# Two mixers of a streaming encoder: three projection blocks between scores and transposes, the product with v one pair later

## The chip, the cores and the metric

The kernel runs on one core of a Trainium2 chip. The metric is the device time of one launch in microseconds, the median of three runs.

## The reference, cut to what matters

The input x is 256 rows of 1024 float32 values. Two layers follow each other; each is FFN, mixer, FFN, with a residual and a layer norm behind each of the three. Every norm needs the whole row, so nothing of the next stage can begin on a row before its norm is done.

```python
x = layer_norm(ALPHA * x + 0.5 * swiglu(x, ...))      # 1024 -> 2816 -> 1024
q, k, v = (x @ w_qkv) cut into 16 heads of 64
# layer 0: softmax(q k^T * scale + bias by clipped distance), band of 64-row chunks
# layer 1: a = sigmoid(z) * product of sigmoid(-z) over later keys, strictly causal
x = layer_norm(ALPHA * x + (a @ v) @ w_o)
x = layer_norm(ALPHA * x + 0.5 * swiglu(x, ...))
```

## The kernel before

Every large product is made in three matmuls for accuracy. A weight is read by DMA into one of four raw slots (L280, L310), ScalarE copies it to a rounded high part (`hi_part`, L605), VectorE subtracts to get the low part (`lo_part`, L773), and TensorE issues high by high, high by low and low by high (`three`, L354). A *unit* is 128x2048 weights; `unit_ready(n)` makes TensorE wait until the low part of unit n is there. Five slots hold the split weights, and a slot is written again once the unit before it in the same slot has been used (`unit_used`). x itself is turned by TensorE (`transpose_x`, L344) and split in the same way (`xT_hi_part` L640, `xT_lo_part` L803), in three pieces for each half of the rows.

In a mixer TensorE works through 24 projection blocks (`proj_block`: 24 matmuls of 128x128 by 256 columns each), 8 pairs of heads, and 16 half blocks of the output product (`out_half`: 6 matmuls of 512 columns). A v block covers 128 rows and all four heads of its group; a q or k block covers one pair of heads and all 256 rows. A block's result goes to one of two PSUM banks and ScalarE copies it out (`copy_proj`, L675); block i waits for the copy of block i - 2. All engines have one fixed order of work, written by hand; semaphores carry the rest.

For a pair of heads the steps are: `scores` (TensorE, L516, banks 0 and 1); then the weights: in mixer 0 VectorE adds the bias and takes the extremes (`soften`, L889), ScalarE takes the exponentials (L685), VectorE divides by the sums (`normalise`, L896 and L901); in mixer 1 ScalarE makes two sigmoids (L693, L696), GpSimd masks both (L1026), VectorE scans (L909) and multiplies (`break_sticks`, L916). Then `turn_probs` transposes the weights into the same two banks (TensorE, L526), ScalarE copies them out (`probsT_copy`, L702), `head_out` multiplies with v (TensorE, L537 and L538), and ScalarE and VectorE split the result (L706, L921).

The order on TensorE before: the blocks v00, v10, v01, v11, q00, k00, q01 (unit, then half), the first pair's scores, and for each pair

```python
scores(m, pp)
todo, turn = fillers(pp)
for j, block in enumerate(todo):
    if j == turn:
        turn_probs(m, pp)
    ...                      # proj_block or out_half
head_out(m, pp)
```

So two blocks lie between the scores and the transposes (three half blocks in the last two pairs), one behind them, and then the product with v of the same pair. Pair 5 has two projection blocks and one half block. VectorE begins a mixer with the norm and split of the second half of the rows (`norm(t - 1, 1, split_too=True)`, L816 to L839 and L803) and only then makes the low parts of the mixer's units 2, 3 and 4, in this order. Units 0 to 3 are v0, v1, q0 and k0; units 0 and 1 were split in the FFN before. When the output product is done, `finish` turns the first half of the new x.

Of the kernel before, what the change touches and what calls it, by code (L numbers as in the profile page):

```python
# [26 lines left out]
P = 128  # L27
SEQ, D, FF, HEADS, HD = 256, 1024, 2816, 16, 64
DEPTH = 2
ROWS = SEQ // P  # L30
# [38 lines left out]

FFN_SLOTS = [j % 4 for j in range(24)] + [4, 0, 1, 2, 3, 0, 4, 2, 3]  # L70
MIX_SLOTS = [0, 1, 4, 2, 3] + [4, 0, 1, 2, 3] * 2 + [4]
SLOT = (FFN_SLOTS + MIX_SLOTS + FFN_SLOTS) * DEPTH
assert len(SLOT) == UNITS and len(FFN_SLOTS) == UNITS_FFN and len(MIX_SLOTS) == UNITS_MIX


def former(n):
# [4 lines left out]

MIX_ORDER = ([("v", 0), ("v", 1), ("q", 0), ("k", 0), ("q", 1), ("k", 1)]
             + [(what, g) for g in range(2, GROUPS) for what in "vqk"] + [("o", g) for g in range(GROUPS)])

BLOCKS = [("v", 0, 0), ("v", 1, 0), ("v", 0, 1), ("v", 1, 1)]
for group in range(GROUPS):
    if group >= 2:
        BLOCKS += [("v", group, 0), ("v", group, 1)]
    BLOCKS += [(what, group, pair) for pair in range(2) for what in "qk"]
FIRST_BLOCKS = 7  # L90

AHEAD = [(6, 7), (8, 9), (10, 11), (12, 13), (14, None), (15, 16), (None, 17), (None, None)]
# [6 lines left out]
def build(nc, x_in, w_qkv, w_o, rel_bias, w_gate, w_up, w_down, ln_g, ln_b, table, out):  # L101
    with ExitStack() as ctx:
# [58 lines left out]
        Y = [[psum[:, 5, :], psum[:, 6, :]], [psum[:, 7, :], psum[:, 3, :]]]  # L161

# [5 lines left out]
        SCORES = psum[:, 0:2, 0:KEYS]  # L168
# [56 lines left out]
        def wait_block(eng, m, i):  # L225

            what, g, b = BLOCKS[i]
            if b == 0:
                eng.wait_ge(proj_done, m * 3 * GROUPS + sum(x[2] == 0 for x in BLOCKS[:i + 1]))
            else:  # L230
                eng.wait_ge(unit_used, MIX_UNIT[m] + MIX_ORDER.index((what, g)) + 1)

        def fillers(pp):


            o = [("o", g, r, half) for g in range(GROUPS) for r in range(ROWS) for half in range(2)]
            if pp < PAIRS - 2:
                at = FIRST_BLOCKS + 3 * pp
                return (BLOCKS[at:at + 3] + o)[:3], 2
            at = 4 * (pp - (PAIRS - 2)) + 1  # L240
            return o[at:at + 4], 3
# [85 lines left out]
        def _(pe):  # L327
# [77 lines left out]
            def half_block(r, half, d, n, count, ready=None):  # L405
# [3 lines left out]
                for kk in range(2):  # L409
# [3 lines left out]
                    last = three(Y[r][half], (hT_hi[:, k, rows], hT_lo[:, k, rows]),  # L413
# [51 lines left out]
            def proj_block(m, i, t=None, between=()):  # L465
# [10 lines left out]
                for k in range(KD):  # L476
# [3 lines left out]
                    if t is not None:  # L480
                        xT_ready(t, b, k)
# [8 lines left out]
            def out_half(m, g, r, half):  # L490

                n = MIX_UNIT[m] + 3 * GROUPS + g
                if half == 0:
                    unit_ready(n)
                if (g, r, half) == (0, 1, 1):

                    pe.wait_ge(proj_copied, (m + 1) * len(BLOCKS))

                last = half_block(r, half, g, n, GROUPS,
                                  lambda kk: pe.wait_ge(headout_lo, m * PAIRS + 2 * g + kk + 1))  # L500
# [5 lines left out]
            def scores(m, pp):  # L506
# [3 lines left out]
                if m * PAIRS + pp > 0:  # L510
                    pe.wait_ge(probsT_done, m * PAIRS + pp)
                q, k = qT[g % 2], kT[g % 2]
                for r, (a, b) in enumerate(SPANS):
                    for h in range(2):
                        part = slice(h * HD, (h + 1) * HD)
                        last = pe.matmul(SCORES[:, h, a:b], q[part, p, r * P:(r + 1) * P], k[part, p, 0:b - a],  # L516
                                         start=True, stop=True)
                last.then_inc(scores_done, 1)

            def turn_probs(m, pp):  # L520
                pe.wait_ge(probs_ready, m * PAIRS + pp + 1)
                pr = probs[pp % 2]
                for h in range(2):

                    for to, at in ((0, 2 * P), (P, 0), (2 * P, P)):
                        last = pe.transpose(SCORES[:, h, to:to + P], pr[:, h, at:at + P], ident[:])  # L526
# [15 lines left out]
            def mixer_matmul(m, t, finish):  # L542
# [4 lines left out]
                for i in range(3, FIRST_BLOCKS):  # L547
                    proj_block(m, i)
                for pp in range(PAIRS):
                    scores(m, pp)  # L550
                    todo, turn = fillers(pp)
                    for j, block in enumerate(todo):
                        if j == turn:
                            turn_probs(m, pp)
                        if block[0] == "o":
                            out_half(m, *block[1:])
                        else:
                            proj_block(m, BLOCKS.index(block))
                    head_out(m, pp)
                last_g = GROUPS - 1  # L560
                out_half(m, last_g - 1, 0, 1)
                for half in range(2):
                    out_half(m, last_g, 0, half)
                for half in range(2):
                    out_half(m, last_g - 1, 1, half)
                out_half(m, last_g, 1, 0)
                finish((0, 1))
                out_half(m, last_g, 1, 1)
# [26 lines left out]
        def _(act):  # L595
# [4 lines left out]
            def hi_part(n, raw_slot, count, slot, before):  # L600

                act.wait_ge(raw_loaded[raw_slot], count * 32)
                if before is not None:
                    act.wait_ge(unit_used, before + 1)
                act.activation(w_hi[slot][:], raw[raw_slot][:], ACT.Copy).then_inc(hi_done, 1)  # L605

            def hi_unit(n):
                if n < UNITS:
                    hi_part(n, n % RAW, n // RAW + 1, SLOT[n], former(n))
# [33 lines left out]
            def ffn_scalar(f, t):  # L643
# [8 lines left out]
                with act.Fori(0, CHUNKS // 2) as i:  # L652
                    for cc in (1, 2):
                        c = i * 2 + cc
                        silu(f, c - 1, 1, (cc - 1) % 2)
                        for kh in range(2):
                            j = 2 * cc + 2 + kh
                            n = n0 + j
                            hi_part(i * 4 + n, n % RAW, i + (n // RAW + 1), j % 4, i * 4 + (n - 4))
# [9 lines left out]
            def copy_proj(m, i):  # L669
                what, g, b = BLOCKS[i]  # L670
                wait_block(act, m, i)
                if g >= 2:
                    act.wait_ge(headout_done, m * PAIRS + 2 * (g - 1))
                dst = {"v": v, "q": qT, "k": kT}[what][g % 2]
# [14 lines left out]
            def sigmoids(m, pp):  # L689
# [3 lines left out]
                act.activation(stick[:], SCORES, ACT.Sigmoid, scale=-1.0).then_inc(sigmoid_done, 1)  # L693
                if pp >= 2:
                    act.wait_ge(probsT_psum, m * PAIRS + pp - 1)
                act.activation(probs[pp % 2][:], SCORES, ACT.Sigmoid).then_inc(sigmoid_done, 1)  # L696

            def probsT_copy(m, pp):
# [3 lines left out]
                act.activation(probsT[:], SCORES, ACT.Copy).then_inc(probsT_done, 1)  # L702
# [342 lines left out]
```

## Time and profile before

| | |
|---|---|
| median of the three runs | 1000.98 us (1000.14, 1000.98, 1001.07) |
| span of the profiled execution | 998.0 us |
| outside the span, against the median | 3.0 us |
| TensorE matmuls | 983.0 us busy, 98% of the span |
| VectorE | 571.9 us, 57% |
| ScalarE | 444.5 us, 45% |
| mixer 0 | from about 196.6 to 309 us |
| mixer 1 | from about 684.5 to 801 us |

For the profiled execution the page has the span from its first to its last instruction and no whole time of its own; the runs' times include what lies before and behind the span, 3.0 us by the median. Matmuls are pipelined and their ends are modelled, so this document compares the starts of matmuls: in a running block of 256-column matmuls they are 0.12 us apart, in a half block of 512 columns 0.23 us.

### The profile page before, as it was taken

The numbers are of one execution on the slowest core, as the hardware profiler recorded it, in microseconds if no ns is written. First come the engines' busy times: TensorE is split into PE (matmuls) and PEld (weight loads), VectorE is DVE, ScalarE is ACT, GpSimd is POOL, SyncE is SP. The second block draws the span as 40 slices with busy tenths as digits, with TensorE's granted clock in tenths as the row PEclk, the third lists the DMA queues.
The fourth block names the chain that finished last, engine by engine and source line by source line (L and its number), as shares of the span: only waits on it lengthen the run. The fifth ranks groups of instructions, "written<-read, shape, count | busy, mean of one in ns | idle before, by whom it ended". The sixth has DMA issues, their size and how long they took to land.

```text
span 998.0 us, 13263 instructions
## 1 busy us (share of the span) xinstructions
PE 983.0 (98%) x5158; PEld 826.3 (83%) x5158; DVE 571.9 (57%) x624; ACT 444.5 (45%) x507; POOL 44.7 (4%) x72
## 2 busy tenths in 40 slices
PE   9999999999999999999999999999999999999996
PEld 7888888899987888888888888889888678888885
DVE  5555463766557555554665554547576585445634
ACT  5443452357653444352254434534565443344430
POOL 1100000000001000000000000001121110000000
PEclk9999999999999999999999999999999999999999
DMA  9956546456633756546565565654554436564521
GB/s 319 290 185 194 199 174 220 166 182 225 211 114 90 247 169 196 188 172 243 169 211 168 180 198 197 225 174 154 180 196 142 127 124 210 181 201 168 210 85 43
DMA packets 136951, 182.80 MB, mean 183 GB/s; under 512 B 5936, under 2 KB 120784, under 8 KB 136912
## 3 DMA queue, kind: packets, MB, share of 16 engines
q1 hardware_dynamic: 134032, 173.56, 52.6%
q0 software_dynamic: 2592, 8.17, 2.6%
q8 instruction: 28, 0.46, 0.2%
q10 hardware_dynamic: 288, 0.52, 0.2%
q14 instruction: 11, 0.09, 0.0%
HBM read 181.16 MB, written 1.07 MB: 183 GB/s over the span
## 4 chain that ended last, share of the span: by engine, by line
PE 91%; DVE 5%; POOL 1%; issue 1%; ACT 1%; DMA 0%; POOLq 0%; SPq 0%; DVEq 0%
PE psum L356 28%; PE psum L358 28%; PE psum L357 28%; PE psum L393 2%; DVE stick L909 2%; PE psum L516 1%; PE psum L526 1%; POOL stick L1026 1%; PE psum L537 1%; PE psum L344 1%; DVE probs L916 1%; DVE stats L819 1%; DVE x L839 1%; DVE x L816 1%; ACT stick L693 1%
## 5 line engine op out<-in xcount | busy, mean ns | idle before, releaser
L773 DVE TENSOR_TENSOR w_lo<-raw,w_hi 128x2048 fp32r<-128x2048 f32 x162 | 368.8, 2287 | 158.0 <-ACT w_hi L605 157.5
L605 ACT ACTIVATE w_hi<-raw 128x2048 fp32r<-128x2048 f32 x162 | 303.0, 1907 | 89.5 <-PE psum L358 87.8
L356 PE MATMUL psum<-w_hi,xT_hi 128*128 128x512 f32 (+1 forms) x832 | 317.2, 381 | 0.7 <-DVE w_lo L782 0.7
L358 PE MATMUL psum<-w_hi,xT_lo 128*128 128x512 f32 (+1 forms) x832 | 310.9, 374 | 0.0
L357 PE MATMUL psum<-w_lo,xT_hi 128*128 128x512 f32 (+1 forms) x832 | 310.4, 373 | 0.0
L356 PEld LDWEIGHTS psum<-w_hi,xT_hi 128*128 128x128 f32 x832 | 156.7, 188 | 29.8 <-DVE w_lo L782 1.8
L358 PEld LDWEIGHTS psum<-w_hi,xT_lo 128*128 128x128 f32 x832 | 156.5, 188 | 28.3
L357 PEld LDWEIGHTS psum<-w_lo,xT_hi 128*128 128x128 f32 x832 | 156.9, 189 | 25.9
L356 PE MATMUL psum<-w_hi,hT_hi 128*128 128x512 f32 x416 | 164.3, 395 | 0.0
L358 PE MATMUL psum<-w_hi,hT_lo 128*128 128x512 f32 x416 | 162.1, 390 | 0.0
L357 PE MATMUL psum<-w_lo,hT_hi 128*128 128x512 f32 x416 | 162.0, 390 | 0.0
L629 ACT ACTIVATE gate_act<-psum 128x256 f32<-128x256 f32 x88 | 33.8, 384 | 255.8 <-PE psum L358 255.8
L790 DVE TENSOR_TENSOR hidden<-psum,gate_act 128x256 f32<-128x256 f32 x88 | 37.3, 424 | 161.6 <-ACT gate_act L629 161.6
L356 PEld LDWEIGHTS psum<-w_hi,hT_hi 128*128 128x128 f32 x416 | 78.1, 188 | 17.2 <-issue 1.7
L358 PEld LDWEIGHTS psum<-w_hi,hT_lo 128*128 128x128 f32 x416 | 78.1, 188 | 16.6
L357 PEld LDWEIGHTS psum<-w_lo,hT_hi 128*128 128x128 f32 x416 | 78.2, 188 | 15.5
L356 PE MATMUL psum<-xT_hi,w_hi 128*128 128x256 f32 x256 | 73.7, 288 | 0.0
L357 PE MATMUL psum<-xT_lo,w_hi 128*128 128x256 f32 x256 | 72.4, 283 | 0.0
L358 PE MATMUL psum<-xT_hi,w_lo 128*128 128x256 f32 x256 | 72.3, 283 | 0.0
L356 PEld LDWEIGHTS psum<-xT_hi,w_hi 128*128 128x128 f32 x256 | 49.0, 191 | 2.7 <-issue 2.0
L357 PEld LDWEIGHTS psum<-xT_lo,w_hi 128*128 128x128 f32 x256 | 49.1, 192 | 0.0
L358 PEld LDWEIGHTS psum<-xT_hi,w_lo 128*128 128x128 f32 x256 | 49.0, 192 | 0.0
(71 smaller groups left out, 512.2 us busy)
## 6 DMA issues: line engine op xcount, KB each, us to landing
raw<-in_ffn_w_down SPq DMA_DIRECT2D x88, 512.0 KB, 4.1
raw<-in_ffn_w_gate SPq DMA_DIRECT2D x86, 512.0 KB, 4.0
raw<-in_ffn_w_up SPq DMA_DIRECT2D x86, 512.0 KB, 5.0
raw<-in_w_qkv_a SPq DMA_DIRECT2D x24, 512.0 KB, 4.7
raw<-in_w_qkv_b SPq DMA_DIRECT2D x24, 512.0 KB, 4.5
raw<-in_w_o_a SPq DMA_DIRECT2D x8, 512.0 KB, 4.1
raw<-in_w_o_b SPq DMA_DIRECT2D x8, 512.0 KB, 3.7
gain<-in_ln_g POOLq DMA_DIRECT2D x6, 512.0 KB, 3.9
```

The lines of the kernel that those rows point to most:

```text
L344: last = pe.transpose(XT(piece)[:, (k - a) * P:(k - a + 1) * P], x[:, r, k * P:(k + 1) * P], ident[:])
L356: pe.matmul(acc, st[0], mv[0], start=first, stop=False)
L357: pe.matmul(acc, st[0], mv[1], start=False, stop=False)
L358: return pe.matmul(acc, st[1], mv[0], start=False, stop=last)
L393: last = pe.transpose(TURN[:, (2 * j + r) * P:(2 * j + r + 1) * P], hidden[:, r, j * P:(j + 1) * P], ident[:])
L516: last = pe.matmul(SCORES[:, h, a:b], q[part, p, r * P:(r + 1) * P], k[part, p, 0:b - a], start=True, stop=True)
L526: last = pe.transpose(SCORES[:, h, to:to + P], pr[:, h, at:at + P], ident[:])
L605: act.activation(w_hi[slot][:], raw[raw_slot][:], ACT.Copy).then_inc(hi_done, 1)
L629: act.activation(gate_act[:, r, :], GU[par][r][:, 0:CHUNK_F], ACT.Silu).then_inc(silu_done, 1)
L773: dve.tensor_tensor(w_lo[slot][:], raw[raw_slot][:], w_hi[slot][:], ALU.subtract).then_inc(lo_done, 1)
L790: dve.tensor_tensor(hidden[:, r, :], GU[par][r][:, CHUNK_F:], gate_act[:, r, :], ALU.mult).then_inc(hidden_done, 1)
L909: dve.tensor_tensor_scan(stick[:, h, ::-1], stick[:, h, ::-1], restart[:, ::-1], 1.0, ALU.mult, ALU.max).then_inc(stick_done, 1)
```

## The change

The order of blocks and pairs is now a table. Three blocks (or two blocks and two half blocks, or six half blocks) lie between a pair's scores and its transposes; behind the transposes come the product with v of the pair before, and the scores of the next pair. Scores alternate between banks 0, 1 and banks 5, 6, and the mixer's output accumulates in banks 7, 2, 3 and 1. Only four blocks stand ahead of the first scores: v00, v10, q00, k00. The units' order of arrival is unchanged up to index 5; later v of a group comes behind its q and k. Weight splits, copies and waits on ScalarE and VectorE are put in the new order.

```diff
+FIRST_BLOCKS = [("v", 0, 0), ("v", 1, 0), ("q", 0, 0), ("k", 0, 0)]
+DURING = [[("v", 0, 1), ("q", 0, 1), ("k", 0, 1)],
+          [("v", 1, 1), ("q", 1, 0), ("k", 1, 0)],
+          [("q", 1, 1), ("k", 1, 1), ("q", 2, 0)],
+          [("k", 2, 0), ("q", 2, 1), ("v", 2, 0)],
+          [("k", 2, 1), ("v", 2, 1), ("q", 3, 0)],
+          [("k", 3, 0), ("q", 3, 1), ("v", 3, 0)],
+          [("k", 3, 1), ("v", 3, 1), ("o", 0, 0, 0), ("o", 1, 0, 0)],
+          [("o", 0, 0, 1), ("o", 0, 1, 0), ("o", 0, 1, 1), ("o", 1, 0, 1), ("o", 1, 1, 0), ("o", 1, 1, 1)]]
+LAST_TURNED = [("o", 2, 0, 0)]
+LAST_OUT = [("o", 2, 0, 1), ("o", 3, 0, 0), ("o", 3, 0, 1), ("o", 2, 1, 0), ("o", 2, 1, 1), ("o", 3, 1, 0)]
...
-AHEAD = [(6, 7), (8, 9), (10, 11), (12, 13), (14, None), (15, 16), (None, 17), (None, None)]
+AHEAD = [(None, 5), (6, 7), (8, 9), (10, 11), (12, None), (13, 14), (15, 16), (17, None)]
...
+        Y_MIX = [[psum[:, 7, :], psum[:, 2, :]], [psum[:, 3, :], psum[:, 1, :]]]
...
-        SCORES = psum[:, 0:2, 0:KEYS]
+        SCORES = [psum[:, 0:2, 0:KEYS], psum[:, 5:7, 0:KEYS]]
...
                     if t is not None:
-                        xT_ready(t, b, k)
+                        xT_ready(t, b if what == "v" else 1, k)
...
-                if m * PAIRS + pp > 0:
-                    pe.wait_ge(probsT_done, m * PAIRS + pp)
+                if pp >= 2:
+                    pe.wait_ge(probsT_done, m * PAIRS + pp - 1)
...
                 proj_block(m, 2, t)
-                for i in range(3, FIRST_BLOCKS):
-                    proj_block(m, i)
+                proj_block(m, 3)
+                scores(m, 0)
                 for pp in range(PAIRS):
-                    scores(m, pp)
...
+                    for todo in DURING[pp]:
...
+                    turn_probs(m, pp)
+                    if pp > 0:
+                        head_out(m, pp - 1)
+                    if pp + 1 < PAIRS:
+                        scores(m, pp + 1)
+                for todo in LAST_TURNED:
+                    out_half(m, *todo[1:])
+                head_out(m, PAIRS - 1)
+                for todo in LAST_OUT:
+                    out_half(m, *todo[1:])
                 finish((0, 1))
-                out_half(m, last_g, 1, 1)
+                out_half(m, GROUPS - 1, 1, 1)
                 finish((2,))
...
                 copy_proj(m, 2)
                 copy_proj(m, 3)
+                weights(m, 0)
                 hi_unit(n0 + 4)
...
+                    for i in blocks[0:1]:
                         copy_proj(m, i)
+                    if during:
+                        hi_unit(n0 + during)
+                    for i in blocks[1:2]:
+                        copy_proj(m, i)
                     if after:
                         hi_unit(n0 + after)
                     for i in blocks[2:]:
                         copy_proj(m, i)
+                    if pp > 0:
+                        headout_hi_part(m, pp - 1)
+                    if m % 2 == 0 or pp + 1 == PAIRS:
+                        probsT_copy(m, pp)
+                    if pp + 1 < PAIRS:
+                        weights(m, pp + 1)
+                        if m % 2 == 1:
+                            probsT_copy(m, pp)
+                headout_hi_part(m, PAIRS - 1)
...
                 norm(t - 1, 1, split_too=True)
-                for n in range(n0 + 2, n0 + 5):
+                for n in range(n0 + 2, n0 + 4):
                     lo_unit(n)
-                before = 5
+                before = None
                 for pp in range(PAIRS):
+                    if pp >= 2:
+                        headout_lo_part(m, pp - 2)
                     if m % 2 == 0:
                         soften(m, pp)
-                    if before and pp < PAIRS - 2:
+                    if before:
                         lo_unit(n0 + before)
                     if m % 2 == 0:
                         normalise(m, pp)
                     else:
                         sticks(m, pp)
                         break_sticks(m, pp)
-                    during = AHEAD[pp][0] if pp < PAIRS - 2 else before
+                    if pp == 0:
+                        lo_unit(n0 + 4)
+                    during, before = AHEAD[pp]
                     if during:
                         lo_unit(n0 + during)
-                    headout_lo_part(m, pp)
-                    before = AHEAD[pp][1]
+                headout_lo_part(m, PAIRS - 2)
+                headout_lo_part(m, PAIRS - 1)
                 norm(t, 0)
```

What is left out: a unit's release is now counted by a table (`uses_done`), since units are no longer used up in the order in which they come; the copies of q and k of groups 2 and 3 wait for scores instead of for the product with v; and the norm behind a mixer reads the new output banks.

## Rows read from the trace of the kernel before

**Rows 1.** The page: span, and its first part (busy time of the engines).

```profile
span 998.0 us, 13263 instructions
PE 983.0 (98%) x5158; PEld 826.3 (83%) x5158; DVE 571.9 (57%) x624; ACT 444.5 (45%) x507; POOL 44.7 (4%) x72
```

**Rows 2.** Waits, mixer 1 (685 to 810 us): total, times, longest.

```profile
PE psum L526 <- DVE probs L916: 4.4, 7, 1.6
```

**Rows 3.** Waits, mixer 0 (190 to 330 us).

```profile
PE psum L344 <- DVE x L839: 0.4, 1, 0.4
```

**Rows 4.** Timeline, mixer 1: start, duration, engine, line; first and sixth pair's transposes.

```profile
712.38 0.28 PE L358 MATMUL psum<-xT_hi,w_lo 128*128 128x256 f32 x1
713.27 0.96 DVE L916 TENSOR_TENSOR probs<-probs,stick 128x766 f32<-128x766 f32 x1
714.28 0.88 PE L526 MATMUL psum<-ident,probs 128*128 128x128 f32 x6 [1.63 <-DVE probs L916]
714.91 0.36 PE L356 MATMUL psum<-xT_hi,w_hi 128*128 128x256 f32 x1
715.11 0.28 PE L357 MATMUL psum<-xT_lo,w_hi 128*128 128x256 f32 x1
...
772.10 0.28 PE L358 MATMUL psum<-xT_hi,w_lo 128*128 128x256 f32 x1
772.22 0.82 PE L526 MATMUL psum<-ident,probs 128*128 128x128 f32 x6
```

**Rows 5.** Timeline, opening of mixer 0: third block and low part of unit 2.

```profile
202.80 0.60 PE L344 MATMUL psum<-ident,x 128*128 128x128 f32 x4
...
203.16 0.36 PE L356 MATMUL psum<-w_hi,xT_hi 128*128 128x256 f32 x1
...
204.07 0.69 DVE L803 TENSOR_TENSOR xT_lo<-psum,xT_hi 128x512 fp32r<-128x512 f32 x1 [1.23 <-ACT xT_hi L640]
...
204.56 0.28 PE L358 MATMUL psum<-w_hi,xT_lo 128*128 128x256 f32 x1
204.68 2.28 DVE L773 TENSOR_TENSOR w_lo<-raw,w_hi 128x2048 fp32r<-128x2048 f32 x1
204.82 0.38 PE L356 MATMUL psum<-w_hi,xT_hi 128*128 128x256 f32 x1
```

**Rows 6.** Timeline, opening of mixer 1: the same two.

```profile
690.98 0.36 PE L356 MATMUL psum<-w_hi,xT_hi 128*128 128x256 f32 x1
...
692.50 2.28 DVE L773 TENSOR_TENSOR w_lo<-raw,w_hi 128x2048 fp32r<-128x2048 f32 x1
```

**Rows 7.** Timeline, mixer 0: end of block q01, first scores, and that block's copy.

```profile
217.74 0.28 PE L358 MATMUL psum<-xT_hi,w_lo 128*128 128x256 f32 x1
217.95 0.93 PE L516 MATMUL psum<-kT,qT 64*128 64x128 f32 x8
218.06 0.38 ACT L675 ACTIVATE qT<-psum 128x256 f32<-128x256 f32 x1 [2.49 <-PE psum L358]
```

**Rows 8.** Timeline, mixer 1: product with v, next pair's scores, mask and scans.

```profile
717.75 0.28 PE L358 MATMUL psum<-xT_hi,w_lo 128*128 128x256 f32 x1
717.96 0.66 PE L537 MATMUL psum<-probsT,v 128*64 128x256 f32 x4
...
718.77 0.93 PE L516 MATMUL psum<-kT,qT 64*128 64x128 f32 x8
...
720.70 1.73 POOL L1026 TENSOR_SCALAR_AFFINE_SELECT stick<-stick 128x512 f32<-128x512 f32 x1 [9.19 <-ACT stick L693]
...
722.46 2.23 DVE L909 TENSOR_TENSOR_SCAN stick<-stick,restart 128x384 f32<-128x384 f32 x2 [0.53 <-POOL stick L1026]
```

**Rows 9.** Timeline: the kernel's last matmul.

```profile
990.08 0.39 PE L358 MATMUL psum<-w_hi,hT_lo 128*128 128x512 f32 x1
```

**Rows 10.** Stretches at the end: stretch, its length, engines' busy time, granted clock, DMA.

```profile
993.50:993.75 0.25, 0.00 (x0) 0.00 (x0) 0.25 (x2) 0.00 (x0) 0.00 (x0) 0.57 0.00 0
```

**Rows 11.** Timeline: the kernel's first matmuls.

```profile
1.62 2.93 PE L585 MATMUL psum<-ident 128*128 128x128 f32 x12 [1.62 <-POOL ident L991]
```

More of the change, by code:

```diff
@@ L67, with last_use @@
 NORM_SCALE = [(2 * ALPHA, 4 * EPS), (ALPHA, EPS), (2 * ALPHA, 4 * EPS)] * DEPTH
+MIX_ORDER = ([("v", 0), ("v", 1), ("q", 0), ("k", 0), ("q", 1), ("k", 1), ("q", 2), ("k", 2), ("v", 2),
+              ("q", 3), ("k", 3), ("v", 3)] + [("o", g) for g in range(GROUPS)])
+FIRST_BLOCKS = [("v", 0, 0), ("v", 1, 0), ("q", 0, 0), ("k", 0, 0)]
+DURING = [[("v", 0, 1), ("q", 0, 1), ("k", 0, 1)],
[7 rows of a table added]
+LAST_TURNED = [("o", 2, 0, 0)]
+LAST_OUT = [("o", 2, 0, 1), ("o", 3, 0, 0), ("o", 3, 0, 1), ("o", 2, 1, 0), ("o", 2, 1, 1), ("o", 3, 1, 0)]
+BLOCKS = FIRST_BLOCKS + [todo for during in DURING for todo in during if todo[0] != "o"]
+OUTS = [todo for during in DURING for todo in during if todo[0] == "o"] + LAST_TURNED + LAST_OUT + [("o", 3, 1, 1)]
+def last_use(unit):
+    uses = [(what, g) for what, g, *_ in BLOCKS + OUTS]
+    return max(i for i, use in enumerate(uses) if use == unit)
+RELEASED = sorted(MIX_ORDER, key=last_use)
 FFN_SLOTS = [j % 4 for j in range(24)] + [4, 0, 1, 2, 3, 0, 4, 2, 3]
@@ L73, with uses_done @@
 assert len(SLOT) == UNITS and len(FFN_SLOTS) == UNITS_FFN and len(MIX_SLOTS) == UNITS_MIX
+def uses_done(n):
+    for at in MIX_UNIT:
+        if at <= n < at + UNITS_MIX:
+            return at + RELEASED.index(MIX_ORDER[n - at]) + 1
+    return n + 1
 def former(n):
     return max((k for k in range(n) if SLOT[k] == SLOT[n]), default=None)
[L82 to L90, printed above, removed]
-AHEAD = [(6, 7), (8, 9), (10, 11), (12, 13), (14, None), (15, 16), (None, 17), (None, None)]
+AHEAD = [(None, 5), (6, 7), (8, 9), (10, 11), (12, None), (13, 14), (15, 16), (17, None)]
 KEYS = 384
@@ L230, in wait_block @@
             else:
[L231 to L241, printed above, removed]
+                eng.wait_ge(unit_used, uses_done(MIX_UNIT[m] + MIX_ORDER.index((what, g))))
         @block.sync
@@ L403, in chunk_in_loop, with half_block @@
                 gate_up(1, par, slot, n, True).then_inc(unit_used, 1)
-            def half_block(r, half, d, n, count, ready=None):
+            def half_block(r, half, d, n, count, ready=None, y=Y):
                 s = SLOT[n]
@@ L412, in half_block @@
                         ready(kk)
-                    last = three(Y[r][half], (hT_hi[:, k, rows], hT_lo[:, k, rows]),
+                    last = three(y[r][half], (hT_hi[:, k, rows], hT_lo[:, k, rows]),
                                  (as_rows(w_hi[s])[:, kk, cols], as_rows(w_lo[s])[:, kk, cols]),
@@ L515, in scores @@
                         part = slice(h * HD, (h + 1) * HD)
-                        last = pe.matmul(SCORES[:, h, a:b], q[part, p, r * P:(r + 1) * P], k[part, p, 0:b - a],
-                                         start=True, stop=True)
+                        last = pe.matmul(SCORES[pp % 2][:, h, a:b], q[part, p, r * P:(r + 1) * P],
+                                         k[part, p, 0:b - a], start=True, stop=True)
                 last.then_inc(scores_done, 1)
@@ L608, in hi_unit @@
                 if n < UNITS:
-                    hi_part(n, n % RAW, n // RAW + 1, SLOT[n], former(n))
+                    before = former(n)
+                    hi_part(n, n % RAW, n // RAW + 1, SLOT[n], None if before is None else uses_done(before))
             def hi_early(parts):
@@ L671, in copy_proj @@
                 wait_block(act, m, i)
-                if g >= 2:
+                if g >= 2 and what == "v":
                     act.wait_ge(headout_done, m * PAIRS + 2 * (g - 1))
+                elif g >= 2:
+                    act.wait_ge(scores_done, m * PAIRS + 2 * (g - 2) + b + 1)
                 dst = {"v": v, "q": qT, "k": kT}[what][g % 2]
```

54 lines of the change are left out of this document (18 added, 36 removed).

## The prediction

> **What bounds the kernel now.** I read the page first. TensorE is busy for 983.0 of 998.0 us, VectorE for 57% [rows 1]. No engine can free more than TensorE's own idle time, so a reordering can only gain what TensorE waits for in the two mixers, and the little that it loses at each change from one kind of work to another. The waits of each mixer came next. In mixer 1, TensorE's transposes wait seven times for the weights, 4.4 us in all [rows 2]; in mixer 0 no transposes wait at all, the only row of TensorE's matmuls is 0.4 us at the turning of x [rows 3]. So the cure is needed in one mixer and is given to both. Last I read the timeline at the places that the new order touches.
>
> A wait in this list is counted from a modelled end. In starts, which is what the path pays, transposes that nothing holds begin 0.12 us after the block's last matmul starts (772.10 to 772.22), those of the first pair 1.90 us after it (712.38 to 714.28) [rows 4]: 1.78 lost where the list says 1.63. I add this 0.16 to each of the seven: 4.44 + 7 x 0.16 = **5.6 us**, all in mixer 1.
>
> **The change part by part.**
>
> *The transposes' wait goes.* A pair's weights in mixer 1 are ready when VectorE's scans end, at 722.46 + 2.23 = 724.69, plus the break of 0.96 [rows 4, 8]: 725.7, that is 6.9 us after the scores began at 718.77 [rows 8]. New cover: scores 0.86, then three blocks of 24 x 0.12 = 2.9 each, 9.5 us in all; with six half blocks (36 x 0.23) 9.1. Slack is over 2 us, so this holds even where the mask shares its time with a low part and takes 1.73, as it does in the row. The first pair waits longest now because ScalarE first copies the high part of unit 5; the new order puts the weights ahead of it. Gain 5.6 us. I followed what is late next: the copy of a pair's transposes (0.81) has a whole pair's time before the product with v wants it; the second bank pair lets the next scores start without it; each weight split in the new table is ready a block or more before its block, the tightest being unit 5 in mixer 0, behind the next pair's bias step. Copies, raw loads on SP's queue and the bias loads on GpSimd's are the same in number and keep several us of room. I cost these at nothing.
>
> *The third block is now q00 instead of v01.* This is the term that decides. v01 used unit 0, split long before. q00 uses unit 2. VectorE makes that low part only behind the norm and the last piece of x: 204.68 to 206.96 [rows 5]. The third block started at 203.16 [rows 5]; it now has to wait for 206.96 and the 0.05 that the transposes took from the break's end (714.23) to their start (714.28) [rows 4]: 207.01. That is 3.85 us of an idle TensorE. Back comes the small wait for x in the middle of the third block (204.56 to 204.82 instead of 0.12: 0.14 us [rows 5]). Mixer 1 has the same picture: 690.98 against 692.50 + 2.28 + 0.05 = 694.83, again 3.85 [rows 6]. The queue behind it is the whole mixer, as TensorE's order is fixed; VectorE does nothing for q00 earlier, since the change moves only unit 4. The fourth block needs unit 3, 2.28 us later, while q00 runs for 2.9: no second wait. Cost 2 x 3.7 = **7.4 us**.
>
> *The first scores follow k00 at once.* Before, block q01 stood between. A copy starts 0.32 after the last matmul's start and takes 0.38; the scores followed at 0.21 [rows 7]. They now wait until 217.74 + 0.32 + 0.38 + 0.05, in the old times 218.49 instead of 217.95: 0.54 per mixer, **1.1 us**. The second pair's scores also want the block just ahead of them (k01), but the transposes lie between: 0.12 + 0.63 gives the same 0.75. Zero.
>
> *Fewer changes of work.* Behind the transposes a block's second matmul comes 0.20 after the first instead of 0.12 (714.91, 715.11) [rows 4]: 0.08 lost. The product with v starts 0.21 after a block instead of 0.12 (717.75, 717.96) [rows 8]: 0.09 lost. Both happen eight times per mixer and go: 8 x 0.17 = 1.36. In their place come seven steps straight from transposes to a product with v and one to scores, which the trace doesn't show. Bounds: free, or as dear as both that go (0.17). I take 0.09, the product's loss behind a block, the nearest row: 0.72. The half block put between the last two products costs one more step in and out, 0.2. Net gain 0.44 per mixer, **0.9 us**; with the bounds 1.16 to -0.2 per mixer.
>
> The same matmuls run otherwise. The mixer's end keeps its order of half blocks from o201 on, with the norm in the same place, so the tail is as before.
>
> **Sum.** -5.6 + 7.4 + 1.1 - 0.9 = **+2.0 us**: mixer 0 +3.8, mixer 1 -1.8. The span of 998.0 becomes 1000.0; 3.0 us lie outside it by the median of the runs (1000.98), so 1003.0. With the bounds of the unseen steps the sum is +0.6 to +3.3. I count 0.2% (2.0 us) as what a measurement of this kernel can tell from no change; the forecast sits on that edge.
>
> **Rivals.** *The clock falls in the new gap.* TensorE's last matmul ends at 990.47 [rows 9], and in the stretch from 993.50 the mean granted clock is 0.57 [rows 10], between full and half, so it fell from 2.4 to 1.2 GHz at about 993.54: after 3.07 us of idleness. The new gap runs from the end of the last turn of x (202.80 + 0.60 = 203.40 [rows 5]) to 207.01: 3.6 us, longer than any now inside the kernel. The nearest work that looks slow is the warm-up: twelve transposes in 2.93 us, about 0.23 each [rows 11], against 0.105 each in mixer 1 (0.63 for six, 714.28 to 714.91) [rows 4]. If a stretch as long, some 2.8 us, is done at that pace, 1.5 us are lost. One fall gives 1004.5, two 1006.0. For it: 3.6 is more than 3.07. Against: one fall is no rule, and it may need luck of timing.
> The Trainium skill (TensorE: Matmul & The Clock Gate, section "HAM oscillation — how this bites in real kernels") says that an idle gap long enough makes the clock drop and the following work start cold. By that rule the time is one of these two, if this gap is long enough, and that no run here shows.
>
> *Faster: q00 finds its low part ready.* If the third block didn't wait, the 7.4 go and the sum is -5.4: 995.6. It decides for faster once the low part comes 2.0 us earlier in each mixer (by about 205.0). For: everything else in the change works. Against: VectorE's queue is strict, and the row has it start at 204.68, right behind the last piece of x; I find nothing in the diff that moves it.
>
> *The change doesn't do what it says.* The weights are still late behind three blocks. Then the 5.6 stay and the time is 1008.6. Against: over 2 us of slack at the mixer where they are late.
>
> **How the numbers follow.** The sum with the clock staying up: 0.45. At least one fall: 0.36. q00 not waiting, or only briefly: 0.07. Weights still late, or another new wait: 0.05. Within the sum's case but with half of the 3.7 missing or doubled: 0.07. The forecast is the first case, 1003.0. Range 1000.8 to 1006.2: from just above the free steps' lower side to two falls; the faster rival and the late weights lie outside, with the rare ends. Chances: slower by over 0.2% takes a bit under half of the first case and nearly all of the falls and late weights, 0.53; within 0.2% 0.39; faster 0.08.
>
> **What would show it.** In the new profile TensorE waits at the third block of each mixer for the low part of unit 2, 3.6 us from the last turn of x; mixer 0 is 3.8 us longer and mixer 1 is 1.8 shorter; no transposes wait in either; the first scores start 0.75 after k00's last matmul instead of 0.21; the product with v comes 0.6 to 0.75 after the transposes begin. A granted clock under 1.00 behind the gap would speak for the second case, together with blocks whose matmuls start over 0.2 apart. Wrong would be: a gap much shorter than 3.6, transposes that wait, or a wait for a copy or a weight inside the pairs.

## The result: 1007.0 us, 0.6% slower, past the range by 0.8 us

| | before | after |
|---|---|---|
| median, six runs each on one chip | 1000.73 us (1000.14 to 1001.07) | 1007.0 us (1004.76 to 1008.41) |
| ratio, 95% interval | | 1.0060 (1.0049 to 1.0071) |
| profiled execution: whole time, span | span 998.0 | 1008.05, span 1006.1 |
| mean granted clock in the profiled execution | 0.998 | 0.991 |

The forecast was 1003.0 with a range of 1000.8 to 1006.2. The kernel became slower, as forecast, but by 6.3 us instead of 2. The runs of after also lie wider apart (3.7 us) than those of before (0.9 us).

The page of after, its span and first part, and the granted clock by slice:

```profile
span 1006.1 us, 13252 instructions
PE 986.4 (98%) x5158; PEld 831.0 (83%) x5158; DVE 572.4 (57%) x624; ACT 444.3 (44%) x507; POOL 43.8 (4%) x72
PEclk9999999989999999999999999999999999999999
```

Beside [rows 1] the matmuls are the same in number and busy 3.4 us longer. A busy time that grows with no work added points to the clock, and one slice of the clock's row, about 201 to 226 us, has an 8.

**The waits that were forecast are there.** Waits of TensorE in after, total, times, longest:

```profile
PE psum L368 <- DVE w_lo L795: 7.2, 2, 3.6
PE psum L531 <- ACT kT L691: 0.9, 2, 0.5
PE psum L356 <- DVE x L862: 0.8, 2, 0.4
```

No row has the transposes (L541) any more; [rows 2] had seven of them. In their place stand two waits of 3.6 us for a low part and two of 0.5 for the copy of k00. Timeline of after at the opening of mixer 0 (start, duration, line, operation; idle time before it and releaser in brackets), to be laid beside [rows 5], and the same place in mixer 1 beside [rows 6]:

```profile
202.91 0.60 PE L356 MATMUL psum<-ident,x 128*128 128x128 f32 x4
...
204.17 0.69 DVE L825 TENSOR_TENSOR xT_lo<-psum,xT_hi 128x512 fp32r<-128x512 f32 x1 [1.23 <-ACT xT_hi L654]
204.78 4.48 DVE L795 TENSOR_TENSOR w_lo<-raw,w_hi 128x2048 fp32r<-128x2048 f32 x2
207.12 0.58 PE L368 MATMUL psum<-xT_hi,w_hi 128*128 128x256 f32 x1 [3.61 <-DVE w_lo L795]
207.49 0.41 PE L369 MATMUL psum<-xT_lo,w_hi 128*128 128x256 f32 x1
207.71 0.41 PE L370 MATMUL psum<-xT_hi,w_lo 128*128 128x256 f32 x1
...
697.67 0.60 PE L356 MATMUL psum<-ident,x 128*128 128x128 f32 x4
...
701.88 0.58 PE L368 MATMUL psum<-xT_hi,w_hi 128*128 128x256 f32 x1 [3.61 <-DVE w_lo L795]
```

The third block starts 4.21 us after the last turn of x instead of 0.36. That is what was predicted, to a few hundredths. Now look at what follows it: the block's own matmuls start 0.37 and 0.22 apart, and about 0.21 from there on, where a running block has 0.12. The stretches around it in mixer 0, then mixer 1 (stretch, length, busy time and count of the five engines, granted clock, DMA share, GB/s):

```profile
200.00:206.00 6.00, 3.50 (x31) 3.27 (x29) 4.41 (x8) 3.79 (x7) 1.11 (x2) 1.00 0.28 104
206.00:207.00 1.00, 0.00 (x0) 0.00 (x0) 1.00 (x2) 1.00 (x1) 0.00 (x0) 0.67 1.01 262
208.00:213.00 5.00, 5.00 (x25) 5.00 (x25) 1.26 (x1) 0.36 (x1) 0.00 (x0) 0.50 1.00 314
213.00:214.00 1.00, 1.00 (x10) 1.00 (x9) 0.00 (x0) 0.02 (x1) 0.00 (x0) 0.92 1.10 350
701.00:702.00 1.00, 0.12 (x1) 0.12 (x1) 1.00 (x2) 1.00 (x1) 0.00 (x0) 0.64 1.01 328
702.00:707.00 5.00, 5.00 (x24) 5.00 (x25) 2.03 (x1) 0.21 (x2) 0.00 (x0) 0.50 0.88 289
```

The clock was at 2.4 GHz (1.00) when TensorE fell idle at 203.51. In the slice from 206.00 it has a mean of 0.67, so it fell to 1.2 GHz (0.50) about 0.34 us into it, at 206.34, after 2.8 us of idleness; [rows 10] had 3.07 us at the kernel's end. It came back 0.16 us into the slice from 213.00. Of these 6.8 us, 6.0 are work at half clock. 24 or 25 matmuls are done in 5 us there, against some 42 at 0.12 apart. In mixer 1 it fell at 701.28, 3.0 us into the idleness.

**Where 8.1 us of span went.** From the first block of a mixer to the first turn of its new x, mixer 0 took 111.02 us before and 117.97 after, mixer 1 116.98 and 118.04. That is +6.95 and +1.06, 8.0 of the 8.1. By parts, in starts:

| term | predicted, per mixer | mixer 0 | mixer 1 |
|---|---|---|---|
| transposes' waits gone | -5.6 (mixer 1 only) | 0 | -5.95 |
| gap before the third block | +3.85 | +3.85 | +3.86 |
| small wait for x in the third block gone | -0.14 | -0.24 | -0.24 |
| first scores behind k00 | +0.54 | +0.55 | +0.55 |
| changes of work (what the other rows leave) | -0.44 | +0.15 | +0.11 |
| third and fourth block at half clock: 8.37 and 8.45 instead of 5.73 from first to last start | 0 in the forecast, +1.5 in rival 1 | +2.64 | +2.72 |

Of the 5.95, 5.55 lie ahead of the seven transposes that were held, in starts; the other 0.4 is that in a held group the second transpose comes 0.06 later. Without the last row the sum is +2.6; the forecast was +2.0 with bounds of 0.6 to 3.3. The last row alone is 5.4 us.

The timeline of after, changes of work in mixer 0 and the first scores, shows two more lines of the forecast:

```profile
215.49 0.28 PE L370 MATMUL psum<-xT_hi,w_lo 128*128 128x256 f32 x1
215.81 0.38 ACT L691 ACTIVATE kT<-psum 128x256 f32<-128x256 f32 x1 [2.79 <-PE psum L370]
216.25 0.93 PE L531 MATMUL psum<-kT,qT 64*128 64x128 f32 x8 [0.47 <-ACT kT L691]
...
247.21 0.28 PE L370 MATMUL psum<-xT_hi,w_lo 128*128 128x256 f32 x1
247.33 0.82 PE L541 MATMUL psum<-ident,probs 128*128 128x128 f32 x6
...
248.07 0.66 PE L552 MATMUL psum<-probsT,v 128*64 128x256 f32 x4
```

The first scores start 215.49 to 216.25 = 0.76 after the last matmul of k00 (predicted 0.75). The product with v starts 248.07 - 247.33 = 0.74 after the transposes, predicted 0.6 to 0.75. A block used to follow them after 0.58, so the unseen step costs 0.16 to 0.17. That is its upper bound, not the 0.09 that I took.

### The profile page after: what moved, and what is told of

It reads as the page before. It is cut to its first block, busy times and chain, and to the rows that moved or that the text cites. A ratio compares the mean times of both kernels' runs of the same rounds, so it can differ in the third digit from the quotient of the medians.

```text
span 1006.1 us, 13252 instructions
## 1 busy us (share of the span) xinstructions
PE 986.4 (98%) x5158; PEld 831.0 (83%) x5158; DVE 572.4 (57%) x624; ACT 444.3 (44%) x507; POOL 43.8 (4%) x72
## 4 chain that ended last, share of the span: by engine, by line
PE 94%; DVE 3%; issue 1%; DMA 0%; POOL 0%; ACT 0%; POOLq 0%; SPq 0%
PE psum L368 30%; PE psum L370 29%; PE psum L369 29%; PE psum L405 2%; PE psum L531 1%; PE psum L541 1%; PE psum L552 1%; PE psum L356 1%; DVE stats L842 1%; DVE x L862 1%; DVE x L838 1%; DMA raw<-in_ffn_w_up 0%; DVE xT_lo L825 0%; DVE w_lo L795 0%; POOL rstd L1005 0%
## 5 line engine op out<-in xcount | busy, mean ns | idle before, releaser
L368 PE MATMUL psum<-xT_hi,w_hi 128*128 128x256 f32 x256 | 76.3, 298 | 7.2 <-DVE w_lo L795 7.2
L369 PE MATMUL psum<-xT_lo,w_hi 128*128 128x256 f32 x256 | 74.8, 292 | 0.0
L370 PE MATMUL psum<-xT_hi,w_lo 128*128 128x256 f32 x256 | 74.7, 292 | 0.0
L368 PEld LDWEIGHTS psum<-xT_hi,w_hi 128*128 128x128 f32 x256 | 51.6, 202 | 11.0 <-DVE w_lo L795 7.7
L369 PEld LDWEIGHTS psum<-xT_lo,w_hi 128*128 128x128 f32 x256 | 51.7, 202 | 0.0
L370 PEld LDWEIGHTS psum<-xT_hi,w_lo 128*128 128x128 f32 x256 | 51.6, 201 | 0.0
```

The lines of the kernel that those rows point to most:

```text
L368: pe.matmul(acc, st[0], mv[0], start=first, stop=False)
L369: pe.matmul(acc, st[0], mv[1], start=False, stop=False)
L370: return pe.matmul(acc, st[1], mv[0], start=False, stop=last)
```

## The experiments

Two theories stood at first. A: the time over the plain sum (the 5.4 us of the table's last row; by the medians the kernel is 4.0 over the forecast) is the clock, brought down by the idle gap, and the plain sum is right. B: the third and fourth block are slow for another reason that lies with them (the transfers beside them, the order of splits), and would be so with a busy TensorE. The diffs below are cut, and against the changed kernel where nothing else is said.

**e1: the gap stays, TensorE is kept busy in it.**

```diff
                 transpose_x(t, 1, (2,))
+                for _ in range(16):
+                    pe.matmul(Y[1][0][:, 0:P], ident[:], ident[:], start=True, stop=True)
                 proj_block(m, 2, t)
```

> The changed kernel with 16 small matmuls of the identity (as in the warm-up, 32 passes, about 0.1 us each, 3.3 us) in the gap ahead of the third block; they compute nothing that is used. Theory (an idle gap lets the clock fall, and the blocks behind it run slowly): the third block starts as late as before, but q00 and k00 take 5.7 us and not 8.4, the granted clock stays up, and the time is the changed kernel's best sum, about 1003.7 (1000.9 + 2.75), with runs close together. Rival (the slow stretch comes from what runs beside it, the loads or the weight split): q00 and k00 still take 8.4 us, 1008.

Measured: 1002.97 us (1002.43 to 1003.53, 7 runs), ratio to before 1.0028 (1.0017 to 1.0040), 2.75 us over the 1000.22 of before in the same batch. Timeline of e1 (L562 is the added work, two records to a matmul):

```profile
203.15 3.74 PE L562 MATMUL psum<-ident 128*128 128x128 f32 x32
206.92 0.39 PE L368 MATMUL psum<-xT_hi,w_hi 128*128 128x256 f32 x1
207.14 0.28 PE L369 MATMUL psum<-xT_lo,w_hi 128*128 128x256 f32 x1
```

and the stretch of its third and fourth block:

```profile
207.00:213.00 6.00, 5.93 (x48) 5.73 (x48) 2.07 (x1) 0.67 (x4) 0.00 (x0) 1.00 0.90 295
```

The third block starts as late as in after (4.21 us behind the last turn of x), the DMA share beside it is the same (0.90, and 0.91 in the same stretch of after) and so is the order of splits, and both blocks take 5.73 us at a clock of 1.00. Theory B is refuted. What is left, 2.75 us, is close to the table's sum without its last row, 2.6.

**e3: the wait without the new order.** The kernel before, with one wait put in (the diff is against it).

```diff
                 transpose_x(t, 1, (2,))
+                unit_ready(MIX_UNIT[m] + 2)
                 proj_block(m, 2, t)
```

> The kernel before, order and all, with one wait added: the third block (v01) waits for the low part of unit 2, which it doesn't read. Theory (the wait and the fall behind it explain the loss): a gap of 4.2 us between the last turn of x and the third block where there was 0.36, so +3.6 per mixer net of the small wait in v01, +7.2, and up to 2.7 more for each fall: 1008.1 without a fall, 1013.5 with two. Rival (the loss comes from the new order of pairs, banks and copies): under 1003.

Measured: 1011.46 us (1010.96 to 1011.73, 4 runs), ratio 1.0112 (1.0095 to 1.0129); the profiled span is 1009.0. Waits of e3:

```profile
PE psum L356 <- DVE w_lo L774: 7.2, 2, 3.6
PE psum L526 <- DVE probs L917: 4.4, 7, 1.6
```

The gap is 4.21 and 4.20 us and the five blocks behind it take 15.85 and 16.74 us instead of 14.58 and 14.60. So the wait alone, with the old blocks behind it, costs 7.7 us of gap and 3.4 us of clock, 11.1 in all; the span grew by 11.0. The time lies between the two that were expected for no fall and for two. With this, neither the bank pairs nor the table of blocks is needed to explain the loss. Both waits of before and after stand here side by side, which shows that the new order removed the one and brought the other.

**e2 and e9: less idleness.** Half and a quarter of e1's filling: 8 matmuls (the diff shows the change to e1) and 4 in place of 16, their results unused as in e1. That leaves 1.82 and 2.72 us idle.

```diff
-                for _ in range(16):
+                for _ in range(8):
```

> The same with 8 of them, about 1.65 us, so that TensorE idles for about 2 us of the 3.6. Theory (it is the length of the idle time that counts): no fall, 1003.7 as with 16. Rival (any wait of some us at this place lets the clock fall): slow blocks in one or both mixers, 1006 to 1009.

> The changed kernel with four small matmuls of the identity in the gap, so that TensorE idles for about 2.7 us of the 3.6. With 1.8 us of idle time the time was 1002.9 in most runs and 1004 to 1004.6 in two of seven; with 3.6 it was 1004.8 to 1008.4. Theory (the longer the idle time, the likelier a fall): between the two, a median of 1004 to 1006. Rival (there is a sharp limit between 1.8 and 3.6): the same as one of the two, 1003 or 1007.

Measured, e2: 1002.92 us (1002.80 to 1004.64, 7 runs), ratio 1.0029 (1.0017 to 1.0041). Five runs lie at 1002.8 to 1003.0, inside the range of e1; the other two, 1003.99 and 1004.64, lie above it. The profiled one is 1003.99, and the extra time is in mixer 1. (The run at 1004.64 has no trace, and its mean clock, 0.997, is also that of runs without extra time, so what it lost is not shown.) The timeline of the profiled one there:

```profile
699.06 0.39 PE L368 MATMUL psum<-xT_hi,w_hi 128*128 128x256 f32 x1 [1.82 <-DVE w_lo L797]
...
700.11 0.33 PE L370 MATMUL psum<-xT_hi,w_lo 128*128 128x256 f32 x1
700.24 0.41 PE L368 MATMUL psum<-xT_hi,w_hi 128*128 128x256 f32 x1
700.45 0.41 PE L369 MATMUL psum<-xT_lo,w_hi 128*128 128x256 f32 x1
```

After 1.82 us of idleness the block starts at full speed, and only some ten matmuls in does the pace change from 0.12 to 0.21. The two blocks take 7.22 us instead of 5.73. In mixer 0 of the same execution the idle time was the same and the clock stayed at 1.00.

e9: 1005.03 us (1004.22 to 1006.35, 4 runs), ratio 1.0049 (1.0034 to 1.0065). In its profile, mixer 0 falls (7.22 us for the two blocks; the pace changes at 208.41, 1.3 us after the restart) and mixer 1 does not (5.73), with 2.72 us idle in both. The rows on the clock for mixer 0 and then mixer 1:

```profile
207.00:213.00 6.00, 5.88 (x36) 5.88 (x37) 2.27 (x2) 0.83 (x3) 0.00 (x0) 0.72 0.91 304
702.00:707.00 5.00, 4.74 (x40) 4.54 (x38) 0.88 (x1) 0.61 (x2) 0.00 (x0) 1.00 1.01 332
```

So at these lengths the same idleness brings a fall in one mixer and none in the other; what decides it is not shown. The price isn't fixed either: 1.5 us in e2 and e9, 2.6 and 2.7 in after. The medians rise with the idle time: for about 0, 1.8, 2.7 and 3.6 us they lie 2.75, 2.70, 4.5 and 6.3 us over those of the kernel before beside them. That speaks for the theory of e9 and against its sharp limit.

**e4: the low part of unit 2 made earlier.** If the gap is the cause, closing it should give the gain. VectorE makes the low part inside the norm, behind the first half of the rows' last piece.

```diff
                     if half == 0 and split_too:
                         xT_lo_part(l + 1, 0, (2,))
+                        if l + 1 in MIX_NORM:
+                            lo_unit(MIX_UNIT[MIX_NORM.index(l + 1)] + 2)
...
-                for n in range(n0 + 2, n0 + 4):
+                for n in range(n0 + 3, n0 + 4):
```

> The changed kernel with the low part of unit 2 made inside VectorE's norm, ahead of the second half's residual, instead of behind the norm. Theory: the norm and the turn of x come 1.9 us later (the high part is there at 196.5, the low part takes 2.28, the residual could start at 196.9), so TensorE waits 1.9 us inside the second block and hardly at the third; both waits are too short for a fall. Against the changed kernel: gap 3.85 becomes 1.9 and no slow blocks, about 999.8, so no slower than the kernel before. Rival (VectorE's delay costs as much as the gap, since x late delays everything by the same): 1003 or more.

Measured: 1002.46 us (1001.92 to 1002.95, 10 runs), ratio 1.0022 (1.0013 to 1.0032). 4.5 us under after, and 2.7 over what I expected, nearer to the rival's 1003. Waits and timeline of e4:

```profile
PE psum L368 <- DVE w_lo L795: 3.4, 2, 1.7
PE psum L356 <- DVE x L864: 3.1, 4, 1.2
```

```profile
204.48 0.36 PE L368 MATMUL psum<-xT_hi,w_hi 128*128 128x256 f32 x1
...
205.25 1.91 ACT L618 ACTIVATE w_hi<-raw 128x2048 fp32r<-128x2048 f32 x1
...
207.19 2.29 DVE L795 TENSOR_TENSOR w_lo<-raw,w_hi 128x2048 fp32r<-128x2048 f32 x1 [1.11 <-ACT w_hi L618]
...
209.54 0.39 PE L368 MATMUL psum<-xT_hi,w_hi 128*128 128x256 f32 x1 [1.71 <-DVE w_lo L795]
```

The third block follows the last turn of x at once. But the fourth is k00, whose unit is the next one: ScalarE has its high part only at 207.16, and VectorE's low part of it ends at 209.48. The gap moved by one block and shrank to 1.7 us, and with the split inside the norm TensorE waits up to 1.2 us for x (0.4 in after). What I had not looked at is that both engines split the weights one after the other, behind the same norm. In ten runs idle times of 1.2 and 1.7 us brought no run that stands out: before, the longest idle time of TensorE in the mixers was 1.63 [rows 4].

**e6: the price of a change of work.** The product with v ahead of the transposes instead of behind them.

```diff
-                    turn_probs(m, pp)
                     if pp > 0:
                         head_out(m, pp - 1)
+                    turn_probs(m, pp)
```

> The changed kernel with the product with v ahead of the transposes instead of behind them. The trace of the changed kernel has 0.75 from the transposes to the product with v where transposes to a block take 0.58. Theory (the 0.17 are paid when transposes are followed by a matmul of plain float32, whichever): transposes then scores 0.75 as with the first pair, product behind a block 0.21, and product to transposes about 0.7 of start to start: 0.1 us more per pair at most, 1004 to 1008 as falls of the clock happen. Rival (the 0.17 belong to the product with v): 0.1 less per pair.

Measured: 1007.78 us (1007.57 to 1008.03, 4 runs), ratio 1.0071 (1.0056 to 1.0086). Its timeline for the second pair shown above:

```profile
246.64 0.28 PE L370 MATMUL psum<-xT_hi,w_lo 128*128 128x256 f32 x1
246.85 0.66 PE L552 MATMUL psum<-probsT,v 128*64 128x256 f32 x4
...
247.66 0.87 PE L541 MATMUL psum<-ident,probs 128*128 128x128 f32 x6
...
248.46 0.93 PE L531 MATMUL psum<-kT,qT 64*128 64x128 f32 x8
```

Block to product 0.21, product to transposes 0.81, transposes to scores 0.80. In after the product came 0.74 behind the transposes, and a block came 0.58 behind them. So the rival is refuted: the step is also paid with scores behind the transposes. By the length of the mixers this order is dearer by 0.85 us in each, about 0.12 per pair. It would not have saved the change.

e6 shows something else. TensorE idles for 3.61 us ahead of the third block in both mixers, as in after. The rows on e6's clock for mixer 0 and then mixer 1:

```profile
208.00:211.00 3.00, 3.00 (x16) 3.00 (x16) 1.71 (x1) 0.00 (x0) 0.00 (x0) 0.50 0.82 256
702.00:702.50 0.50, 0.48 (x4) 0.49 (x5) 0.50 (x1) 0.34 (x2) 0.00 (x0) 1.00 0.61 246
703.00:706.00 3.00, 3.00 (x16) 3.00 (x16) 1.16 (x1) 0.00 (x0) 0.00 (x0) 0.50 0.97 309
```

Here the clock fell only when the block had begun (207.57 and 702.01), 0.1 and 0.6 us into it, and was back after 3.4 us; the third and fourth block take 7.23 and 7.21 us. So the same gap cost 1.5 us per mixer here and 2.6 and 2.7 in after. Both happen in e3: half clock for 3.4 us in mixer 0 and for 6.8 in mixer 1.

**e5, e7, e8: does the new order pay once the gap is gone?** In e5 the blocks v01 and v11, whose units were split long before, stand again ahead of q00 and k00; the three-block spacing, the bank pairs and the late product stay. (Its other tables move up with them.)

```diff
+FIRST_BLOCKS = [("v", 0, 0), ("v", 1, 0), ("v", 0, 1), ("v", 1, 1), ("q", 0, 0), ("k", 0, 0)]
...
+          [("v", 3, 1), ("o", 1, 0, 0), ("o", 0, 0, 1), ("o", 0, 1, 0)],
+          [("o", 0, 1, 1), ("o", 1, 0, 1), ("o", 1, 1, 0), ("o", 1, 1, 1), ("o", 2, 0, 0)]]
```

> The changed order of pairs with the early order of before: v01 and v11 go back ahead of q00 and k00, six blocks stand ahead of the first scores, the other blocks and half blocks move up, and the last three pairs get five half blocks' worth of cover. Theory (all of the loss sits at the opening): no gap, no fall, the transposes wait nowhere: -5.8 for the waits, +1.1 for the first scores right behind k00, +0.4 for the changes of work, so 4.3 under the kernel before, about 996. Rival (three blocks between need the late v blocks, and something else waits when they are early): 999 or more.

Measured: 1000.84 us (999.54 to 1001.38, 11 runs), ratio 0.9999 (0.9990 to 1.0008). The opening is as before (the third block 0.35 after the last turn of x) and no transposes wait. Yet 5 us of the expected gain are missing, and the waits name a line that neither before nor after has, a half block that waits for a copy. Wait and timeline of e5, last pair of mixer 1:

```profile
PE psum L368 <- ACT probsT L719: 2.7, 2, 2.3
```

```profile
779.05 0.93 PE L531 MATMUL psum<-kT,qT 64*128 64x128 f32 x8
...
781.43 0.82 ACT L719 ACTIVATE probsT<-psum 128x768 f32<-128x768 f32 x1
782.29 0.79 PE L368 MATMUL psum<-w_hi,hT_hi 128*128 128x512 f32 x1 [2.31 <-ACT probsT L719]
```

Half block ("o", 0, 1, 1) accumulates in bank 1, which holds the transposes of the pair before until ScalarE has copied them out; in mixer 1 that copy comes behind both sigmoids of the last pair. In after another half block stood first. I had put this one at the head of its stretch. TensorE stands still for 2.3 us, and its clock falls 0.5 us before that ends: the 30 matmuls take 8.09 us from first to last start, where the same 30 take 6.71 in mixer 0. So the rival's time came true, but by a fault in my table; that early v blocks need such a wait is refuted by e8.

e7 adds q01 ahead of the first scores, so that the copy of k00 is hidden too (against e5; later blocks move up again):

```diff
-FIRST_BLOCKS = [("v", 0, 0), ("v", 1, 0), ("v", 0, 1), ("v", 1, 1), ("q", 0, 0), ("k", 0, 0)]
+FIRST_BLOCKS = [("v", 0, 0), ("v", 1, 0), ("v", 0, 1), ("v", 1, 1), ("q", 0, 0), ("k", 0, 0), ("q", 0, 1)]
```

> As the one with six blocks, with q01 too ahead of the first scores, so that the copy of k00 is hidden. Theory: 1.1 under that, about 995. Rival (17 blocks and 9 half blocks are too little cover for the last pairs of mixer 1): a wait of up to 1 us in each of the last two, and no gain over six blocks.

Measured: 999.98 us (998.65 to 1000.45, 11 runs), ratio 0.9990 (0.9981 to 0.9999). The scores start 0.21 after the block again. The wait on bank 1 is unchanged, and so is a fall beside it, here 1.3 us behind the wait's end. I expected 995; e7 has the same fault as e5. e8, against e7, puts the two half blocks that write bank 1 behind the two that don't, nothing else:

```diff
-          [("o", 0, 1, 1), ("o", 1, 1, 0), ("o", 1, 1, 1), ("o", 2, 0, 0)]]
+          [("o", 1, 1, 0), ("o", 2, 0, 0), ("o", 0, 1, 1), ("o", 1, 1, 1)]]
```

> The order with seven blocks first, with one exchange in the last pair's half blocks: the half block of rows 128 to 255, columns 512 to 1023 (bank 1, which held the scores of the pair before) comes third and not first. Its wait for the copy of the transposes cost 0.4 us in mixer 0 and 2.4 in mixer 1, and 1.4 more in slow matmuls behind it. Theory: those 4.2 us go, about 996 against 1000.8, and no transposes wait. Rival (the copy of the last transposes or ScalarE's last weights become the bound, so the wait moves to the next step): 998.5 or more.

Measured: **996.62 us** (996.11 to 997.18, 5 runs), ratio 0.9962 (0.9949 to 0.9976): 0.4% faster than the kernel before, and faster than the changed one. The stretch behind the last pair's scores in mixer 1, e7 and then e8:

```profile
784.00:788.00 4.00, 4.00 (x12) 3.08 (x12) 2.62 (x3) 1.91 (x1) 0.00 (x0) 0.61 0.22 79
```

```profile
784.00:788.00 4.00, 4.00 (x26) 3.02 (x26) 2.53 (x3) 2.38 (x3) 0.00 (x0) 1.00 0.09 27
```

The clock is at 0.61 in e7 and at 1.00 in e8. (The counts don't compare: e8's 26 hold small transposes and products.) The same work, from the last pair's scores to its transposes, takes 10.45 us in e7 (779.17 to 789.62) and 6.43 in e8 (779.43 to 785.86). In e8's profile mixer 1 is 5.0 us shorter than before (112.01 against 116.98) and mixer 0 is 1.0 longer (111.98 against 111.02), where there was nothing to cure; together -4.0, and the span went from 998.0 to 994.1. Of the +1.0 in mixer 0, and of the 1.0 by which mixer 1 falls short of 5.95, 0.4 each is the last product's wait for the split of the result ahead of it:

```profile
PE psum L552 <- DVE hT_lo L948: 0.8, 2, 0.4
```

Another 0.2 each is the second half block behind that product, which starts as the next low part ends (0.43 after the matmul ahead of it instead of 0.23). The rest, about a third of a microsecond in each mixer, stays open. An order that leaves mixer 0 as it was and gives only mixer 1 the three blocks was not tried.

## Why the prediction was right and wrong

**Right:** the bound (TensorE's own idle time); that the transposes' waits go entirely (5.6 predicted; 5.55 measured by the same reckoning, and 0.4 more in the transposes themselves) and that only mixer 1 gains; that q00 waits for the low part of unit 2, at 3.85 and 3.86 us per mixer for a predicted 3.85; the first scores (0.54 predicted, 0.55 measured); the net sign. The rivals "q00 finds its low part ready" and "the weights are still late" are refuted by the rows of waits.

**The step that failed** is the choice between the first case and rival 1: the forecast "with the clock staying up" was given 0.45, the fall 0.36. The argument against the fall was "one fall is no rule". The clock fell in both mixers of the profiled execution, after 2.8 and 3.0 us of idleness. e1 shows that the idleness is the cause: the same gap with a busy TensorE costs nothing more than the sum. The row at the kernel's end [rows 10] should have been believed: 3.07 us there, and the new gap was half a microsecond longer. The forecast put the fall at nothing because that was a single row. It did happen in both mixers of all three traces with such a gap (after, e3, e6). With TensorE kept busy the forecast would have stood: e1 is at 1002.97.

**The price within rival 1** was the second error, a mis-sized term. 1.5 us for each fall came from taking the twelve transposes of the warm-up, some 2.8 us, for the whole slow stretch [rows 11]. In the profiled execution of after 6.0 us of work were done at half clock before it rose, and a fall cost 2.64 and 2.72. With that price two falls on the forecast's own sum give 1003.0 + 5.4 = 1008.4, and the profiled run had 1008.05. The row of the warm-up was only the first part of a slow stretch. The timeline of before goes on behind it:

```profile
4.34 1.07 PE L344 MATMUL psum<-ident,x 128*128 128x128 f32 x4
5.64 1.12 PE L344 MATMUL psum<-ident,x 128*128 128x128 f32 x4
```

Four such transposes take 0.60 at full pace [rows 5]. Those at 6.55 us are still 0.21 apart, so the slow pace lasts 5 us and more from the first matmul at 1.62; by the 0.44 that is lost of each slow microsecond (0.213 against 0.12) that is 2.2 us, an estimate, and not 1.5. Still, 1.5 is what each fall of e6 cost behind the same gap. Which price a fall has in a given run, the gap doesn't decide; that the two falls of after's profiled execution were dear ones was not to be foreseen from rows of before. The six runs of after show the spread: two, 1004.76 and 1004.8, lie inside the range, at mean clocks of 0.997 and 0.996 against 0.991 to 0.994 in the longer ones. That fits with fewer or shorter falls, as e9 and e6 have them; for these runs there is no trace.

The Trainium skill (TensorE: Matmul & The Clock Gate, section "HAM oscillation — how this bites in real kernels") describes this: an idle gap brings the clock down and the next piece of work starts cold. The trace agrees for the gap of 3.6 us in after, at a clock of 0.50. It differs in e2 and e9, where the work started at full speed behind 1.82 and 2.72 us of idleness and went slow 1.2 to 1.3 us later, in one mixer and not in the other, and in e6's mixer 1, where it went slow 0.6 us later.

**Changes of work** was the third, and small: -0.9 predicted, about +0.3 measured. The unseen step from transposes to the product with v has the price of its upper bound, 0.17, and I took 0.09. The bounds of 0.6 to 3.3 for the sum held (2.6).

The range ended at 1006.2 because two falls at 1.5 us ended at 1006.0. With the price measured in after it would have reached past 1008 and held the result. Its lower end, 1000.8, was called just above the lower side of the free steps; that side is 1000.98 + 0.6 = 1001.6, so the end lies below it. That changed nothing here.

## What to carry to other kernels

When a block is moved forward to give another wait more cover, ask when its own operands end on the slowest queue that works in order, here VectorE's behind the norm, and ask it for each block that moves up: e4 mended the first and met the second. A new idle gap of TensorE is priced twice: its own length, and a fall of the clock. In these runs a fall cost 1.4 to 2.7 us. The traces show none at 1.7 us of idleness and less (before, e4), one in two mixers at 1.82 (e2) and at 2.72 (e9), one in each of the two at 2.31 (e5 and e7, mixer 1), and six in six at 3.6 (after, e3, e6). A new order has a new first waiter in every stretch (e5, e7: a half block on a bank not yet copied out); putting there a half block that needs nothing made the difference between a gain of 0.8 us (e7) and one of 3.9 (e8), each against the kernel before beside it.

## What was not expected of the hardware

- The clock can fall when the idleness is already over: e2, 1.82 us idle, then 1.2 us of matmuls at full pace, then half clock. The same idle length in the other mixer brought none, and five of seven runs show no lost time. After 3.61 us idle, e6 still had 0.1 and 0.6 us of the next block at full clock. Nor is there a fixed time into the idleness: 2.8 and 3.0 us in after, 3.6 and 2.2 in e3, behind gaps of the same length.
- How long the clock stays low differs: 6.8 us in both mixers of after and in e3's mixer 1, 3.4 us in e2, e9, e5, e7, e3's mixer 0 and both mixers of e6. Only the part with work in it costs: 6.0 us of work at half clock cost 2.6 us in after, 3.4 us cost 1.5 in e2, e6 and e9, and 3.0 cost 1.4 in e5.
- At half clock a block's matmuls of 256 columns start 0.213 us apart, 1.8 times the 0.12 at full clock, not twice.
